# A fused two-block transformer kernel: first-layer input by one combined factor, residual on GpSimd, four projections in split form, pool branch inside attention

## The reference

```
x = first_block(...)                      # ends with rms_norm(x2, g_final)
for l in range(2):
    h = rms_norm_2(x, attn_norm_g[l])
    proj = h @ w_in[l]                    # 1024 x 4768
    c_q, c_kv, k_rope, gq, gk, gv, pool_in, gate_logits = split_columns(proj, IN_SIZES)
    o_mla  = mla_branch(...)              # 8 heads of 96, k and q normalised, rope
    o_gqa  = gqa_branch(...)              # 8 heads of 64, 2 key heads, head norms, rope
    o_pool = pool_branch(pool_in, ...)    # window means 2, 4, 8, 16, then 4 products 128x128
    gates = sigmoid(gate_logits)          # 3 x 1024
    merged = gates0 * (o_mla @ w_b_mla) + gates1 * (o_gqa @ w_b_gqa) + gates2 * (o_pool @ w_b_pool)
    x = x + merged @ w_out[l]
    hf = rms_norm_2(x, ffn_norm_g[l])
    u = depthwise_conv(hf @ ffn_w_up[l], ...)
    x = x + (silu(u_gate) * u_val) @ ffn_w_down[l]
```

## Time and profile before

| | us |
|---|---|
| median of 3 runs | 2143.99 (2139.35 to 2150.68) |
| the profiled execution | 2143.75 |
| its span | 2142.0 |
| PE busy | 2037.8 (95%) |
| DVE busy | 895.1 (42%) |
| ACT busy | 628.8 (29%) |
| POOL busy | 49.3 (2%) |
| mean granted PE clock | 0.988 of full speed |

### The profile page before, as it was taken

One profiled execution on the slowest core, in us unless ns is written; L12 is line 12 of the kernel. 1 busy time (PEld: TensorE's weight loads), 2 busy tenths in 40 slices (PEclk: granted clock), 3 DMA queues, 4 the chain that ended last, 5 costly groups with the idle time before them and its releaser, 6 DMA issues.

```text
span 2142.0 us, 31712 instructions
## 1 busy us (share of the span) xinstructions
PE 2037.8 (95%) x12278; PEld 1305.9 (61%) x12279; DVE 895.1 (42%) x1608; ACT 628.8 (29%) x967; POOL 49.3 (2%) x57
## 2 busy tenths in 40 slices
PE   6999999999999999999999999999999999999999
PEld 4864333333333333333333488879999888789999
DVE  3522221112212221222122446866785348766874
ACT  1421111111111110111111215554654144644553
POOL 0000000000000000000000020000000020000000
PEclk9998999999999999999999999999999999999999
DMA  9785999399999999999589673413655454334563
GB/s 353 265 335 237 417 417 408 133 416 417 418 419 418 417 417 418 419 417 417 210 336 418 257 196 119 139 59 106 209 193 163 140 156 131 117 99 153 169 200 109
DMA packets 222040, 580.35 MB, mean 271 GB/s; under 512 B 23520, under 2 KB 142048, under 8 KB 185984
## 3 DMA queue, kind: packets, MB, share of 16 engines
q1 hardware_dynamic: 221952, 579.09, 71.2%
HBM read 577.74 MB, written 1.31 MB: 270 GB/s over the span
## 4 chain that ended last, share of the span: by engine, by line
PE 70%; DMA 12%; SPq 8%; DVE 5%; ACT 3%; issue 2%; ACTq 0%; DVEq 0%
PE bank L1080 13%; DMA ring<-in_w_gu 9%; PE bank L1136 8%; PE bank L807 6%; SPq L680 4%; SPq L682 4%; PE bank L1427 3%; PE bank L1428 3%; PE bank L1429 3%; PE bank L1032 3%; PE bank L1046 3%; PE bank L1211 2%; PE bank L1212 2%; PE bank L877 2%; PE bank L1213 2%
## 5 line engine op out<-in xcount | busy, mean ns | idle before, releaser
L1080 PE MATMUL bank<-ring,heap 128*64 128x512 f32 x2176 | 491.3, 600 | 31.0 <-DMA ring<-in_w_gu 31.0
L1080 PEld LDWEIGHTS bank<-ring,heap 128*64 128x64 f32 x2176 | 148.4, 137 | 356.9 <-issue 262.4
L2048 DVE TENSOR_SCALAR heap<-bank 128x256 f32<-128x256 f32 (+1 forms) x72 | 26.7, 412 | 724.1 <-PE bank L1080 695.3
L1136 PE MATMUL bank<-ring,heap 128*64 128x512 f32 (+1 forms) x1152 | 255.1, 595 | 0.0
L1427 PE MATMUL bank<-h_hi,w_hi 128*128 128x256 f32 x640 | 181.7, 284 | 2.3 <-DVE w_lo L2324 2.3
L2324 DVE TENSOR_TENSOR w_lo<-ring,w_hi 128x2048 fp32r<-128x2048 f32 (+1 forms) x64 | 142.4, 2225 | 98.7 <-ACT w_hi L1742 98.7
L1428 PE MATMUL bank<-h_lo,w_hi 128*128 128x256 f32 x640 | 181.1, 283 | 0.0
L1429 PE MATMUL bank<-h_hi,w_lo 128*128 128x256 f32 x640 | 181.1, 283 | 0.0
L1578 ACT ACT_TABLE_LOAD x32 | 41.1, 1283 | 470.4 <-DVE heap L2048 468.7
L1136 PEld LDWEIGHTS bank<-ring,heap 128*64 128x64 f32 (+1 forms) x1152 | 78.7, 135 | 150.7 <-issue 145.0
L1742 ACT ACTIVATE w_hi<-ring 128x2048 fp32r<-128x2048 f32 (+1 forms) x64 | 119.1, 1861 | 146.3 <-PE bank L1429 86.0
(11 more groups left out here) (340 smaller groups left out, 3090.1 us busy)
## 6 DMA issues: line engine op xcount, KB each, us to landing
ring<-in_w_gu SPq DMA_DIRECT2D x256, 1024.0 KB, 19.2
ring<-in_w_down SPq DMA_DIRECT2D x128, 1024.0 KB, 21.8
ring<-in_ffn_w_up SPq DMA_DIRECT2D x44, 1024.0 KB, 7.7
ring<-in_w_in SPq DMA_DIRECT2D x32, 1024.0 KB, 5.6
ring<-in_w_ada SPq DMA_DIRECT2D x24, 1024.0 KB, 10.5
ring<-in_ffn_w_down SPq DMA_DIRECT2D x16, 1024.0 KB, 5.1
ring<-in_w_out SPq DMA_DIRECT2D x8, 1024.0 KB, 5.0
ring<-in_w_in SPq DMA_DIRECT2D x3, 2048.0 KB, 26.5
```

The source lines that it names most:

```text
L1080: last = mm(psum[g][both[f], :], xgT[:, k % 4, k // 4, :], wt[:, g, :, :, f, :].rearrange("p i c n -> p (i c) n"), start=False, stop=k == ...
L1136: last = mm(psum[2][FEW * f:FEW * f + n, :], hidT[:, o:o + n], wt[:, 512 * f:512 * (f + 1)], start=k == 0, stop=k == DT - 1)
```

## The change

Entry to the second block: DVE forms xgain in one step from x2, by the combined factor gain0 = g_final * attn_norm gain. ACT squares x2 scaled by g_final. The residual xT = x2 * g_final is made by POOL, behind its folding, and DVE waits for it (xin_ready) before it writes into cq, which lies in the place of x2.

Layer head: gq1, po0, gk and po1 become split products with h (new pieces 0 to 3 of `early_unit`, so the gate pieces are 4 to 15, and so on), in the order gq1, po0, gv, gk, po1. Their first two high parts come before r1's square root on ACT, their first two low parts before r1's chain on DVE. The high and low parts of h are made in two halves. w_po0 moves ahead of w_gkv in the ring, so it too is loaded in the layer before.

Later: the low part of ga8 (now number 12) moves before a product of rope. In attention the low part of the second branch piece moves from the fifth head to behind the last one. The branches go in the order pool, gqa, mla, and 42 of the 48 products of the first one (pool, first half) go into steps 16 and 17 of the attention loop.

```diff
-NG, NB, NW = 12, 6, 22
+NI, NG, NB, NW = 4, 16, 6, 26
+BR = (2, 1, 0)
+FIRST = ("w_gq1", "w_po0", "w_gkv", "w_po1")
...
-        layer = [("w_lat", 8 * 416), ("w_gq0", 8 * 256), ("w_gq1", 8 * 256), ("w_gkv", 8 * 384), ("w_po0", 8 * 256),
-                 ("w_po1", 8 * 256), ("ga0", 8 * 256), ...
+        layer = [("w_lat", 8 * 416), ("w_gq0", 8 * 256), ("w_gq1", 8 * 256), ("w_po0", 8 * 256),
+                 ("w_gkv", 8 * 384), ("w_po1", 8 * 256), ("ga0", 8 * 256), ...
...
 PE
+                def split_steps(out, w, cols, x, ks, nk):
+                    hi, lo = w
+                    for k in ks:
+                        wh, wl = hi[:, k, cols:cols + P], lo[:, k, cols:cols + P]
+                        mm(out, wh, x[0][:, k, :], start=k == 0, stop=False, skip_group_check=True)
+                        mm(out, wh, x[1][:, k, :], start=False, stop=False, skip_group_check=True)
+                        last = mm(out, wl, x[0][:, k, :], start=False, stop=k == nk - 1, skip_group_check=True)
+                    return last
+
+                def by_unit(name, n):
+                    done("wlo", n + 1)
+                    b = halves(lay(name))
+                    for a in range(2):
+                        last = split_tile(b[:, a, :], early_unit(n)[2:], P * a, (h_hi, h_lo), DT, n == 0 and a == 0)
+                    last.then_inc(lay_full.sem, 1)
...
-                for i in range(2):
-                    arrived(f"w_gq{i}")
-                    tiles(f"gq{i}", piece(lay_stream, f"w_gq{i}", 8), 0, raw)
+                arrived("w_gq0")
+                tiles("gq0", piece(lay_stream, "w_gq0", 8), 0, raw)
+                by_unit("gq1", 0)
+                by_unit("po0", 1)
                 arrived("w_gkv")
...
-                for i in range(2):
-                    arrived(f"w_po{i}")
-                    tiles(f"po{i}", piece(lay_stream, f"w_po{i}", 8), 0, h)
+                by_unit("gk", 2)
+                by_unit("po1", 3)
...
+                    if 2 * NH <= i < 2 * NH + 2:
+                        r = i - 2 * NH
+                        pooled[r] = halves(lay(f"br{r}{BR[0]}"))
+                        for a in range(2):
+                            split_steps(pooled[r][:, a, :], early_unit(NG)[2:], 2 * P * r + P * a, (o_hi[2], o_lo[2]),
+                                        range(3 if a else 4), 4)
...
 ACT
-                act.wait_ge(xin_ready.sem, 2 * i + 2)
-                f(L["sq"][:, 2 * i:2 * i + 2, :], xT[:, 2 * i:2 * i + 2, :], ACT.Square).then_inc(S["sq1"].sem, 1)
+                f(L["sq"][:, 2 * i, :], hT[:, 2 * i, :], ACT.Square, scale=v1("g_final", 2 * i))
+                f(L["sq"][:, 2 * i + 1, :], hT[:, 2 * i + 1, :], ACT.Square, scale=v1("g_final", 2 * i + 1)) \
+                    .then_inc(S["sq1"].sem, 1)
...
                 f(L["rs"][:, 1, :], c2, ACT.Sqrt).then_inc(S["std1"].sem, 1)
+                lead(0)
+                lead(1)
                 ready("var1")
...
 DVE
+            c.step(v.tensor_tensor(gain0, gains[:, 0, :], v1("g_final"), ALU.mult))
...
-                if 1 <= k <= DT:
+                if k >= 1:
                     dve.wait_ge(x2_ready.sem, k)
-                    v.tensor_scalar(xT[:, k - 1, :], hT[:, k - 1, :], v1("g_final", k - 1), None, ALU.mult) \
-                        .then_inc(xin_ready.sem, 1)
-                if k >= 2:
-                    dve.wait_ge(xin_ready.sem, k - 1)
-                    v.tensor_scalar(xgain[:, k - 2, :], xT[:, k - 2, :], gains[:, 0, k - 2:k - 1], None, ALU.mult) \
+                    v.tensor_scalar(xgain[:, k - 1, :], hT[:, k - 1, :], gain0[:, k - 1:k], None, ALU.mult) \
                         .then_inc(S["xg"].sem, 1)
...
                 ready("vecs")
+                rest_early(0)
+                rest_early(1)
                 r1 = L["rs"][:, 0, :]
...
+                if l == 0:
+                    dve.wait_ge(xin_ready.sem, DT)
                 taken(by_token(L["cq"], two(full("cq"))))
...
+                for i in range(2):
+                    ready("hhi", i + 1)
+                    v.tensor_tensor(h_lo[:, 4 * i:4 * i + 4, :], L["h"][:, 4 * i:4 * i + 4, :],
+                                    h_hi[:, 4 * i:4 * i + 4, :].bitcast(F32), ALU.subtract).then_inc(S["h1"].sem, 1)
...
-                taken(by_token(L["gq"][:, 2:4, :], two(full("gq1"))))
-                taken(by_token(L["gk"], two(full("gk"))))
+                taken(v.tensor_copy(L["gq"][:, 2:4, :], two(full("gq1"))))
+                rest_early(2)
+                rest_early(3)
+                taken(v.tensor_copy(L["gk"], two(full("gk"))))
...
+                rest_early(12)
                 c.mark(v.tensor_tensor(mk, mk, cos, ALU.mult))
-                rest_early(8)
...
-                    if i < 5:
-                        rest_early(9 + i)
+                    if i < 4 or i == 2 * NH + 1:
+                        rest_early(13 + min(i, 4))
...
 POOL
                 fold("sq1")
+                if l == 0:
+                    for k in range(DT):
+                        pool.wait_ge(x2_ready.sem, k + 1)
+                        g.tensor_scalar(xT[:, k, :], hT[:, k, :], v1("g_final", k), None, ALU.mult) \
+                            .then_inc(xin_ready.sem, 1)
```

More of the change, by code:

```diff
@@ L332, in build @@
         lay_stream = Stream(layer, LRING, again=True)
-        LAY_LAST = {"w_lat": "ckv", "w_gq0": "gq0", "w_gq1": "gq1", "w_gkv": "gv", "w_po0": "po0", "w_po1": "po1",
+        LAY_LAST = {"w_lat": "ckv", "w_gq0": "gq0", "w_gkv": "gk",
                     "w_uq": "uq3", "w_ukv": "uv1", "pool_w": "pl1", "up0": "up1"}
@@ L502, in build @@
         heads = [f"m{h}" for h in range(NH)] + [f"g{h}" for h in range(NH)]
-        order = [("ss1", "dve"), ("cq", "dve"), ("ckv", "dve"), ("gq0", "dve"), ("gq1", "dve"), ("gk", "dve"),
-                 ("gv", "act"), ("po0", "act"), ("po1", "act"), ("sslat", "dve"), ("ssgq", "dve"),
+        order = [("ss1", "dve"), ("cq", "dve"), ("ckv", "dve"), ("gq0", "dve"), ("gq1", "dve"), ("po0", "act"),
+                 ("gv", "act"), ("gk", "dve"), ("po1", "act"), ("sslat", "dve"), ("ssgq", "dve"),
                  ("ssgk", "dve"), ("ga0", "act"), ("ga1", "act")]
@@ L522, in build @@
                 order.append((f"o_{att[i - 4]}", "dve"))
[L523 removed]
+        order += [(f"br{2 * h + r}{b}", "dve") for h in range(2) for b in BR for r in range(2)]
         order += [(f"wo{i}", "dve") for i in range(4)] + [("ss2", "dve")]
@@ L1214, in split_tile @@
                     return last
-                def gates(n):
-                    done("wlo", n + 1)
-                    b = halves(lay(f"ga{n}"))
-                    for a in range(2):
-                        last = split_tile(b[:, a, :], early_unit(n)[2:], P * a, (h_hi, h_lo), DT)
-                    last.then_inc(lay_full.sem, 1)
+                def by_unit(name, n):
[4 more added lines that the diff above has]
+                    last.then_inc(lay_full.sem, 1)
+                def gates(n):
+                    by_unit(f"ga{n}", NI + n)
                 raw = lambda k: xgain[:, k, :]
@@ L1655, in _ @@
                 ready("h1")
-                f(h_hi[:, :, :], L["h"], ACT.Copy).then_inc(S["hhi"].sem, 1)
+                for i in range(2):
+                    f(h_hi[:, 4 * i:4 * i + 4, :], L["h"][:, 4 * i:4 * i + 4, :], ACT.Copy).then_inc(S["hhi"].sem, 1)
+                full("gq1")
+                lead(2)
+                out_of("po0", L["pool"][:, 0:2, PAD:PAD + T])
+                lead(3)
+                out_of("gv", L["gv"], lambda b: two(b)[:, :, 0:P])
+                full("gk")
+                lead(4)
                 out_dve("gk")
@@ L2290, in _ @@
                 for h in range(2):
-                    for br in range(3):
+                    for j, br in enumerate(BR):
                         for i in (2 * h, 2 * h + 1):
```

101 lines of the change are left out of this document (54 added, 47 removed).

## The result

| | before | after |
|---|---|---|
| median, us | 2146.83 (2139.35 to 2150.68, 4 runs) | 2124.45 (2123.67 to 2125.60, 4 runs) |
| the profiled execution, its span | 2143.75, 2142.0 | 2125.60, 2123.8 |
| ratio, 95% interval | | 0.9901 [0.9879, 0.9922] |

The account below looks back on a forecast made before the run. TensorE, busy 95% of the span, bounds the kernel; gains come from fewer PE passes or its waits. 9.1 + 1.15 + 2 x (1.47 + 0.9 + 1.4) = 17.8, less 0.5, takes 2143.75 to 2126.5 us; range 2118 to 2136.

Parts of the forecast that it names:

- Part 1: Layer heads: four projections in split form, 6.90 to 5.76 us per unit, 4.56 per layer, 9.1 us in two layers.
- the 1.4 us to spare: Layer 0 head: h's low halves ready before PE ends gq0, so no stall, with 1.4 us of margin.
- the charge of 0.5: Layer 1 head: 0.5 us deducted because weights land later and h's first low half comes late; bounds 0 and 3.
- Part 2: Entry to the second block: shorter x chain on DVE, middle instruction moved to POOL, everything behind it 1.15 us earlier.
- The limit of 1.99 us per instruction: POOL's eight residual products at the entry: no cost below 1.99 us each; at 2.88 each, 7.1 us lost.
- Parts 3 and 4: ga8's low part before the rope product, 1.47 us per layer; one low part fewer inside attention, 0.9 us per layer.
- rival (a): Attention gives nothing, since a DVE-PE loop or DVE backlog sets the time: 10 us gain left, 2134 us; chance 0.12.
- Part 5: Attention tail: 42 pool branch products cover PE waits of 1.05 and 0.37 us; 1.4 us per layer, bounds 0.5 and 2.
- Rival (c): New order changes the low-clock stretch, 1.7 us per layer: gone in both gives 2123, one more per layer 2130; chance 0.10.
- Rival (b): Layer head stalls: h_lo or first low parts 2 to 3 us late in both layers, 2131 us; chance 0.12.
- (d): Slower: POOL's per-partition product far slower; at 4.2 us each the gain is gone, at 6.5 us 2163; chance 0.06.
- the signs named ahead: Expected in the trace, among others: no PE wait for h_lo above 1 us, at most 0.5 us at each transpose group.

Follow-up runs that it names:

- p1_split_only: Changed kernel with only the split projections and the new branch and ring order, the other timed parts undone: 2135.1 us, ratio to before 0.9955.
- head_low1_later: Changed kernel with po0's low part moved behind the chain of r on DVE: layer 1's head 71.4 us instead of 72.7.
- u2_dve_residual: Changed kernel with DVE making the residual again, ACT squaring the residual, no POOL products: entry stage back at 10.7 us, against 10.1 in after.
- u3_ga8_low_late: Changed kernel with ga8's low part put back behind the rope product: attention stage 98.8 us against 97.3, in both layers.
- u4: Changed kernel with the second branch piece's low part put back into the attention loop: attention stage 98.4 us against 97.3, in both layers.
- u5: Changed kernel with all first-branch products behind the attention loop, new branch order kept: attention stage 98.4 us against 97.3, in both layers.
- pool_two_times: Changed kernel with one extra copy of each POOL residual product, 16 instructions for 8: layer 0's stage from cq to uk 73.5 us against 71.4.
- the run with 24: Changed kernel with each POOL residual product made three times, 24 instructions for 8: layer 0's stage from cq to uk 83.0 us against 71.4.

## Why the prediction was right, step by step

| step | forecast gain, us | measured | by |
|---|---|---|---|
| 1, split units, layer 0 | 4.56 | 4.6 | stages, p1 |
| 1, split units, layer 1 | 4.56 - 0.5 | 3.3 | stages, head_low1_later |
| 2, entry | 1.15 | 0.7 (0.8 as a mean, 0.97 at ACT's last square) | u2 |
| 3, ga8's low part | 2 x 1.47 | 2 x 1.5 | u3 |
| 4, one low part out of the loop | 2 x 0.9 | 2 x 1.1 | u4 |
| 5, branch in the tail | 2 x 1.4 | 2 x 2.3 | u5 1.1, order 1.2 |
| wait for w_lat before layer 1 | none | 1.5 | stage; not tested |
| **sum** | **17.3** | **20.0** (with 0.1 elsewhere) | |

**Part 1** held, in both heads of p1_split_only as well; what w_po0's earlier place in the ring and the halves of h give by themselves was not tested. The unit times are as forecast; taking gq1 and po0 in layer 0 (DVE, then ACT):
```profile
1248.15 0.69 DVE L2207 COPY heap<-bank 128x512 f32<-128x512 f32 x1 [3.17 <-PE bank L1228]
```
```profile
1253.91 0.60 ACT L1655 ACTIVATE heap<-bank 128x512 f32<-128x512 f32 x1 [3.84 <-PE bank L1228]
```
They are 5.76 us apart. There is no wait in layer 0, with the 1.4 us to spare that pool_two_times measured. In layer 1 the charge of 0.5 was too small. The timelines of ACT, DVE and PE there:
```profile
1679.01 1.91 ACT L1668 ACTIVATE w_hi<-ring 128x2048 fp32r<-128x2048 f32 x1 [1.51 <-DMA ring<-in_w_in]
```
```profile
1680.96 2.29 DVE L2172 TENSOR_TENSOR w_lo<-ring,w_hi 128x2048 fp32r<-128x2048 f32 x1 [1.07 <-ACT w_hi L1668]
1683.17 0.42 DVE L2178 SCALAR_TENSOR_TENSOR heap<-bank,vec 128x256 f32<-128x256 f32 x1
```
```profile
1693.22 0.36 PE L1226 MATMUL bank<-h_hi,w_hi 128*128 128x256 f32 x1 [1.04 <-DVE h_lo L2202]
```
The mechanism is the one forecast: w_po0 lands late, its high part waits for it, its low part waits for that, and r's chain stands behind it on DVE. PE came 1.04 us too early, and the whole step is 1.3 us dearer than layer 0's, which head_low1_later takes back by moving that one instruction. The charge was too small because PE came sooner, behind a w_lat that landed sooner (below). Counted from the issue of w_lat (1671.11 in before, 1662.73 in after), the forecast has w_po0 landed after 17.2 us and PE ready for gq1 after 30.9. In after it is 16.3 and 29.5: PE came 1.4 us sooner than forecast, and w_po0 only 0.9.

**Part 2** held within 0.2 to 0.4 us, on the low side of the 1.15 forecast. The entry on DVE and POOL in after:
```profile
1216.46 1.10 DVE L2128 TENSOR_SCALAR heap<-heap,vec 128x256 f32<-128x256 f32 x1
1217.49 0.47 DVE L2123 SCALAR_TENSOR_TENSOR heap<-bank,heap,xT 128x256 f32<-128x256 f32 x1
1217.88 1.87 DVE L2128 TENSOR_SCALAR heap<-heap,vec 128x256 f32<-128x256 f32 x2
```
```profile
1216.14 2.65 POOL L2460 TENSOR_TENSOR heap<-heap 128x512 f32<-128x512 f32 x2 [1215.31 <-ACT heap L1638]
...
1219.58 7.34 POOL L2467 TENSOR_SCALAR xT<-heap,vec 128x256 f32<-128x256 f32 x8
```
One collision with POOL's folding stands ahead of the eighth tile, as assumed, and stretches an instruction of 0.35 us to 1.10, longer than its like in before (0.96). The eighth tile begins 7.64 us behind the combination instead of 8.61.

POOL's products I had taken at 0.7 us each, the far end at 2.88; it is 0.92, the cost 0, and the last ends at 1226.9, 7.6 us before it is needed. The limit of 1.99 us per instruction was not the right picture: what counts is 0.92 per instruction and one block of 3.7 us, once the queue reaches DVE's low parts. The changed kernel is nearer to it than the sum tells: its eighth product begins at 1226.00, 0.3 us ahead of the low parts, and takes its 0.92, and the two tiny sums right behind it are the ones that are held. In after, and under it the same two in the run with 24, where DVE is past its low parts:
```profile
1226.89 4.06 POOL L2472 TENSOR_TENSOR heap<-consts_sb 128x32 f32<-128x32 f32 x2
```
```profile
1243.35 0.44 POOL L2474 TENSOR_TENSOR heap<-consts_sb 128x32 f32<-128x32 f32 x2
```
Nothing waits for these two. The Trainium skill names this contention (GPSIMD Engine Reference, Specifications: GpSimd's SBUF interfaces are shared with VectorE, and instructions of VectorE with two SBUF inputs contend with it). The trace agrees for the fp32 subtraction with two inputs, 4.63 us against 0.92. One reading of the forecast there was inexact: the POOL sum of 1.27 us was not alone, it ran beside the DVE instruction that was stretched to 1.39. The sums that ran alone took 1.29.

**Parts 3 and 4** held to within 0.2 us per layer; rival (a), that attention gives nothing, is refuted by u3, u4 and u5 one at a time. **Part 5** has the right mechanism with a low size, outside its bounds of 0.5 to 2: the hidden waits in the value groups are 1.1 us and not 0.37, and the wait for the last head that the new order covers is worth 1.2.

The **1.5 us before layer 1** were not in the sum: PE's wait there for w_lat (L1232) was 1.8 us in before's profile and is 0.2 in after's, and at most 0.8 in any profile of a changed kernel. The transfer itself was slower. From issue to landing in before (L737), and in after (L742):
```profile
DMA to landing us min/median/max: 8.4/8.4/8.4
```
```profile
DMA to landing us min/median/max: 6.8/6.8/6.8
```
In the other eleven profiles of changed kernels it is 6.8 to 7.4 us, while PE reaches this product 6.7 us behind the issue in before and in after alike. Why it took 8.4 is open: there is one profile of before only, so it may be a difference between executions as well. Rival (c), the clock gone or doubled by the new order, is refuted in its cause: the low stretch is there in both layers of after, as it was in before, and the number of its steps changes between executions of one kernel. Its size, 1.6 us per step against the 1.7 worked out, was right. Rival (b) came true in part, 1.3 us in layer 1 alone, and (d) not at all. Two of the signs named ahead were not met: PE's wait for h_lo in layer 1 is 1.04 us where none above 1 was to be seen, and the transposes in the tail wait 1.34 us where at most 0.5 was.

That 2126.5 was met so closely owes something to chance. The terms are 2.7 us too small together, the last combination of the experts came 1.8 us later in the profiled execution of after, and the base of the sum was an execution 3.1 us below the median that four executions of before give. Against the medians the gain is 22.4 us and not 17.3; the stages account for 20.0 of it, and the rest lies within the scatter of before, 2139.35 to 2150.68 us.

## What to carry to other kernels

Compare by stages that start behind the noisy part of a kernel; here a gain of 1 us per layer is plain in a stage and lost in a scatter of 8 us of the whole. A group of matmuls that is longer than its like at the same clock can hold a wait that no list of waits names, and the yardstick is the shortest group of that kind, not its neighbour. Work added to the idle POOL was nearly free as long as it began before DVE's two long two-input instructions and ended before it was needed; the one product that began beside them paid 3.7 us.

## What the runs showed of the hardware

- GpSimd's product of 128x256 fp32 with a per-partition factor takes 0.92 us. Begun beside two DVE instructions of 128x2048 with two inputs, one of them lasts 4.63 us and ends 0.7 us behind the second; the next ones take 0.92 again. One that began 0.3 us before them (after) kept its 0.92. Two sums of 128x32 that began beside them took 1.82 and 2.28 us instead of 0.23, each ending within 0.2 us of the end of one of the two DVE instructions.
- DVE's two instructions took 4.51 to 4.55 us together with POOL at work, and 4.49 without (u2_dve_residual), so they lost at most 0.1 us. Two short ones of 128x256 behind them (L2181, L2183) took 0.48 and 0.59 us beside POOL's products in pool_two_times, for 0.29 and 0.42 in after.
- The granted clock drops in steps: behind the same tiny matmuls PE spent about 3.3 us at 1.2 GHz, or none, or twice as much, in one kernel's executions too. Each step costs 1.6 us. After 1.47 us of idle PE in p1_split_only there was one such step, while the same wait in u3_ga8_low_late (1.46) and in before (1.47) had none. What decides this is open.
